# Three-product weight halves for the RWKV columns, branch projections and output projection of a hybrid decoder trunk, with constant matmuls at the norms

## The reference

```python
def swiglu(x, wg, wu, wd):
    return (jax.nn.silu(x @ wg) * (x @ wu)) @ wd
...
    for l in range(DEPTH):
        h = swiglu(rmsnorm(x, P['ffn1_pre_g'][l]), P['ffn1_wg'][l], P['ffn1_wu'][l], P['ffn1_wd'][l])
        x = x + 0.5 * rmsnorm(h, P['ffn1_post_g'][l])
        m, new = token_mix(rmsnorm(x, P['mix_pre_g'][l]), l, P, lb[l], s_rwkv[l], s_shift[l], s_lru[l], s_conv[l], s_hgrn[l])
        x = x + rmsnorm(m, P['mix_post_g'][l])
        h = swiglu(rmsnorm(x, P['ffn2_pre_g'][l]), P['ffn2_wg'][l], P['ffn2_wu'][l], P['ffn2_wd'][l])
        x = x + 0.5 * rmsnorm(h, P['ffn2_post_g'][l])
...
# token_mix
    proj = u @ P['w_in'][l]
    pa, pb, pc, pg = jnp.split(proj, [A_PROJ, A_PROJ + 2 * B_WIDTH, A_PROJ + 2 * B_WIDTH + 2 * C_KWIDTH + 2 * C_WIDTH], axis=-1)
...
    ga, gb, gc = jnp.split(jax.nn.sigmoid(pg), 3, axis=-1)
    merged = ga * (oa @ P['proj_a'][l]) + gb * (ob @ P['proj_b'][l]) + gc * (oc @ P['proj_c'][l])
    return merged @ P['w_out'][l], (n_rwkv, n_shift, n_lru, n_conv, n_hgrn)
```

## Time and profile before

| | |
|---|---|
| median of 3 runs | 2296.34 us (2294.59 to 2296.5) |
| the profiled execution | 2293.74 us, its span 2291.8 us |
| PE busy | 2158.2 us (94%) |
| DVE busy | 1142.8 us (50%) |
| ACT busy | 662.9 us (29%) |
| mean DMA rate | 110 GB/s |
| granted TensorE clock, mean | 0.976 of 2.4 GHz |

### The profile page before, as it was taken

One profiled execution on the slowest core, in us unless ns is written; L12 is line 12 of the kernel. 1 busy time (PEld: TensorE's weight loads), 2 busy tenths in 40 slices (PEclk: granted clock), 3 DMA queues, 4 the chain that ended last, 5 costly groups with the idle time before them and its releaser, 6 DMA issues.

```text
span 2291.8 us, 29515 instructions
## 1 busy us (share of the span) xinstructions
PE 2158.2 (94%) x11960; PEld 1812.0 (79%) x11960; DVE 1142.8 (50%) x1787; ACT 662.9 (29%) x751; POOL 35.9 (2%) x72
## 2 busy tenths in 40 slices
PE   7999899999999997999889997999999999979997
PEld 6999667777766766999889996677776666669996
DVE  5443435776557424444354534366754664254533
ACT  4443231211141203443334333212211321034332
POOL 0000000000000000000000000000000000000000
PEclk9999999999999998999999998999999999989998
DMA  5444231111222332444334442311112323324342
GB/s 196 146 150 162 78 125 59 49 65 47 79 95 95 111 110 94 158 151 150 126 140 155 146 162 78 112 42 66 47 65 79 104 85 112 111 100 157 146 158 85
DMA packets 37624, 251.98 MB, mean 110 GB/s; under 512 B 4672, under 2 KB 4864, under 8 KB 8864
## 3 DMA queue, kind: packets, MB, share of 16 engines
q1 hardware_dynamic: 32688, 234.60, 28.5%
q0 software_dynamic: 4848, 16.13, 1.9%
HBM read 242.05 MB, written 8.67 MB: 109 GB/s over the span
## 4 chain that ended last, share of the span: by engine, by line
PE 84%; DVE 9%; ACT 3%; DVEq 3%; issue 1%; DMA 1%; ACTq 0%; SPq 0%
PE dps L471 41%; PE dps L408 15%; PE dps L425 12%; DVE tmp L997 2%; PE mx L562 2%; PE mx L556 2%; PE mx L564 2%; PE mx L438 1%; ACT tmp L761 1%; DVE x L1000 1%; ACT L761 1%; DVE wlo L994 1%; PE mx L670 1%; PE mx L680 1%; DVEq L1397 1%
## 5 line engine op out<-in xcount | busy, mean ns | idle before, releaser
L994 DVE TENSOR_TENSOR wlo<-raw,whi 128x2048 fp32r<-128x2048 f32 x136 | 311.5, 2292 | 398.6 <-ACT whi L761 391.2
L471 PE MATMUL dps<-uh,whi 128*128 128x320 f32 x1408 | 430.5, 306 | 30.6 <-DVE ul L994 30.6
L471 PE MATMUL dps<-uh,wlo 128*128 128x320 f32 x1408 | 436.9, 310 | 0.0
L471 PE MATMUL dps<-ul,whi 128*128 128x320 f32 x1408 | 435.7, 309 | 0.0
L425 PE MATMUL dps<-u,raw 128*128 128x320 f32 x1280 | 407.7, 445 | 0.0
L761 ACT ACTIVATE whi<-raw 128x2048 fp32r<-128x2048 f32 x136 | 259.8, 1912 | 325.0 <-PE dps L471 325.0
L471 PEld LDWEIGHTS dps<-uh,whi 128*128 128x128 f32 x1408 | 267.1, 190 | 33.1 <-issue 32.6
L425 PEld LDWEIGHTS dps<-u,raw 128*128 128x128 f32 x1280 | 226.8, 193 | 70.0 <-issue 11.9
L471 PEld LDWEIGHTS dps<-uh,wlo 128*128 128x128 f32 x1408 | 267.4, 190 | 0.0
L471 PEld LDWEIGHTS dps<-ul,whi 128*128 128x128 f32 x1408 | 266.6, 189 | 0.0
L471 PE MATMUL dps<-hfh,whi 128*128 128x320 f32 x704 | 221.1, 314 | 0.0
(11 more groups left out here) (249 smaller groups left out, 2229.0 us busy)
## 6 DMA issues: line engine op xcount, KB each, us to landing
raw<-in_wstream SPq DMA_DIRECT2D x220, 1024.0 KB, 4.8
hs<-in_st_hgrn POOLq DMA_DIRECT2D x8, 512.0 KB, 3.6
out_o_hgrn<-hsn POOLq DMA_DIRECT2D x8, 512.0 KB, 2.9
sw<-in_smallw POOLq DMA_DIRECT2D x2, 1024.0 KB, 7.1
ss<-in_st_rwkv POOLq DMA_DIRECT2D x8, 256.0 KB, 4.0
out_o_rwkv<-ssn POOLq DMA_DIRECT2D x8, 256.0 KB, 2.3
x<-in_xT SPq DMA_DIRECT2D x4, 320.0 KB, 4.2
out_yT<-x SPq DMA_DIRECT2D x1, 1280.0 KB, 4.5
```

The source lines that it names most:

```text
L471: m = pe.matmul(dps[:, 2 * half + c, 0:T], w[:, k, c * P:(c + 1) * P], v[:, k0 + k, :], start=first and k == 0 and i == 0, stop=last and k ...
L994: return nc.vector.tensor_tensor(out, a, b, op)
```

## The change

1. The A columns, the branch projections and the output projection go from the full to the split form. The unit of splitting is a **half**: half a block, 8 products, 1024 numbers per partition. There are 34 halves in a layer (0 and 1 the low-rank inputs, 2 to 13 r, k and v, 14 to 25 the branch projections, 26 to 33 the output). `high` copies a half on ACT, `low_half` subtracts on DVE, `half_tiles` and `product` multiply. Rounded and low parts go to rooms in tensors that are idle then, four halves deep: `high` of half h waits until half h-4 has been multiplied. A raw buffer is now free for the next block when its second half has been subtracted. `merged`, `oa`, `ob` and `oc` are split as well; `oa` and `ob` inside the HGRN2 heads, `oc` behind the last head, where also the first four halves of the projections are split. The mixer's `norm_in` now makes `uh` and `ul` too.
2. `keep_busy(n)` puts n matmuls of constants (128 by 256 columns, float32, into a bank that nobody reads then) on PE before and after the norm sums in front of the FFNs and of the mixer.
3. In the first FFN, the first block is rounded before the root instead of after it.

The work of the B, C and gate columns is unchanged. The diff, cut to these parts:

```diff
+            def product(out, h, k, n0, src, first, last):
+                wh, wl = split_half(h)
+                hi, lo_ = src
+                for i, (w, v) in enumerate(((wh, hi), (wh, lo_), (wl, hi))):
+                    m = pe.matmul(out, w[:, k, n0:n0 + P], v[:, k, :], start=first and i == 0,
+                                  stop=last and i == 2, skip_group_check=True)
                 return m
+            def half_tiles(l, h, fresh=False):
+                j, c = half_block(h)
+                pe.wait_ge(S["half_lo"], l * NHALF + (h + 1))
+                if c == 0:
+                    pair_wait(l, (Q_A + j - B_A) // 2, j % 2)
+                for k in range(KD):
+                    if fresh and k % 2 == 0:
+                        u_wait(l, 1, k)
+                    m = product(dps[:, 2 * (j % 2) + c, 0:T], h, k, 0, (uh, ul), k == 0, k == KD - 1)
+                m.then_inc(S["half_done"], 1)
+            def keep_busy(n):
+                for _ in range(n):
+                    pe.matmul(mx[:, 0, 0:2 * P], ident, cst[:, 0:2 * P], start=True, stop=True)
...
+                start = l == f == 0
+                keep_busy(0 if start else 12)
                 norm_sum(l, 4 * f)
+                keep_busy(14 if start else 8)
...
+                keep_busy(12)
                 norm_sum(l, 2)
+                keep_busy(11)
+                for h in range(H_A):
+                    half_tiles(l, h, fresh=h == 0)
...
+            def high(l, h):
+                j, c = half_block(h)
+                if c == 0:
+                    act.wait_ge(w_loaded[j % 2], (l * (NBLK // 2) + j // 2) * 16 + 16)
...
+                if 4 <= h < H_PROJ or h >= H_PROJ + 4:
+                    wait_half(act, l, h - 4)
+                fn(split_half(h)[0], full_half(h), ACT.Copy).then_inc(S["half_hi"], 1)
...
+            def low_half(l, h):
+                hi, lo_ = split_half(h)
+                dve.wait_ge(S["half_hi"], l * NHALF + (h + 1))
+                if h == H_PROJ + 1:
+                    dve.wait_ge(S["ss_free"], (l + 1) * HP + 1)
+                elif h == H_PROJ + 2:
+                    wait_full(dve, l, B_PROJ - 1)
+                tt(lo_, full_half(h), hi.bitcast(F32), ALU.subtract).then_inc(S["half_lo"], 1)
...
+                for h in range(H_PROJ, H_PROJ + 4):
+                    low_half(l, h)
+                low_branch(l, 2)
+                for h in range(H_PROJ, H_OUT):
+                    br, i, part = (h - H_PROJ) // 4, (h - H_PROJ) % 4, h % 2
+                    k = slice(2 * i, 2 * i + 2)
+                    wait_half(dve, l, h)
+                    dst = merged[:, k, :] if br == 0 else xs[:, 0:2, :]
+                    mul(dst, dps[:, 2 * part:2 * part + 2, 0:T], gate[:, 8 * br + 2 * i:8 * br + 2 * i + 2, :])\
+                        .then_inc(pair_free[part], 1)
...
+                    if br == 2 and i > 1:
+                        low_merged(i - 2)
+                    if br < 2 or i < 3:
+                        low_half(l, h + 4)
+                low_merged(2)
+                low_merged(3)
...
+                if start:
+                    squares(l, 0)
...
+                    split_hi(l, 0, 0, 0, f)
+                    root(l, 0)
+                    split_hi(l, 0, 1, 1, f)
```

335 lines of the change are left out of this document (217 added, 118 removed).

## The result

The changed kernel takes **2255.95 us** (median of 4 runs, 2255.02 to 2257.43) against 2296.22 of the kernel before on the same chip: ratio 0.983, 95% interval 0.9817 to 0.9844. The profiled executions have spans of 2253.2 and 2291.8 us. So 40.3 us are gained by the medians and 38.6 by the spans, where 46.9 were forecast; the time lies in the forecast range, 7 us above the predicted 2249.

A forecast was written before the change was run, and what follows sets the result against it. PE was taken as the bound, with 84% of the chain. Terms 18.7 + 22.4 + 3.5 + 2.3 = 46.9 us off 2293.74 gave 2246.8; with 2.6 for the median, 2249 us, range 2238 to 2264.

The forecast's parts named there:

- The pace of the products: In the changed stages: split products take 0.440 us instead of 0.538, at most 53 us over 544 products.
- A columns: Mixer's stretch from first u to first attention product: gains of 8.9 and 9.8 us in the two layers, together 18.7.
- The one stall that the walk through the queues had found: A columns: PE waits 1.3 us before half 2, whose slot's copy stands behind `high` of half 4 and table loads.
- Projections and output: Branch and output projections after the last head: gain of 11.2 us a layer, 22.4 in all.
- the other ten halves end at 833.2: Projections, after the 3.5 us stall behind half 15: remaining projection halves finish at 833.2, at 3.52 us of PE each.
- First block ahead of the root: Start of the first FFN: reciprocal comes earlier than 18.24 when the first block is copied before the root; 3.5 us.
- Constant matmuls: Around norm sums: gain of 2.3 us, 1.1 at layer 0's FFN2, 0.2 at two other starts, 1.0 at the first FFN.
- The rule of the Trainium skill: Low-clock penalty at three later FFN starts: would give back 6.3 us instead of 1.3; the prediction set it aside.
- The constant matmuls did not lose the clock or run late: Rival, 4%: at half clock, constant matmuls push norm sums and first products by up to 5 us at five places: 2274.
- The queues do not couple further: Rival, 15%: late low-rank reads in A and the projections lose 4 to 9 us a layer: 2257 to 2267.
- DVE the pace of the projections: Rival "Slower", 2%: DVE's work per half becomes the pace in projections and output, 40 us lost there: 2312.
- More comes back: Rival, 12%: low clock counts by its full share, or the loop's pace holds and stalls fill: 2236 to 2243.

The follow-up runs named there:

- the fifth run: Changed kernel with ScalarE's three decay-constant functions and their table loads moved between the mixer norm's root and the copies of u: 2254.54 us, ratio 0.9823.
- The sixth run: Changed kernel with 8 constant matmuls on PE ahead of half 16, order on DVE and ACT unchanged: 2254.43 us, ratio 0.9823.
- The third run: Changed kernel with DVE's gate multiplications of halves 14 and 15 ahead of later weight subtractions and the low part of `oc`: 2247.15 us, ratio 0.9793.
- The seventh run: Changed kernel with the first FFN's first block copied behind the root again, as in the kernel before: 2260.84 us, ratio 0.9852.
- The ninth run: 15 constant matmuls instead of 8 at three later FFN starts, against a kernel combining gates first, early table loads and earlier low parts of `merged`: 2238.67 us.
- the eleventh: Six constant matmuls in each layer's first HGRN2-head pause, on a kernel with gates first, early tables, earlier `merged`, second-block subtraction behind the norm: 2230.47 us, ratio 0.9723.
- the fourth run: Changed kernel without the third matmul (low weights by high activations) of each product in the new stages: 2212.43 us, one run.

## Why the prediction was nearly right, and which term was too large

**The pace of the products.** 0.1467 us a record was measured, as forecast, and the full form costs 0.542 a product. Right.

**A columns: forecast 8.9 and 9.8 us, measured 8.5 and 8.85.** The one stall that the walk through the queues had found is there, with its size (1.30 us) and its cause, which the fifth run shows: with the table loads ahead of `u` it closes and A is 1.54 and 1.59 us shorter. Over both layers 1.35 us are missing. Half 0 ends 8.1 us after the first u in layer 0 and not 7.8; the rest is not assigned.

**Projections and output: forecast 11.2 us a layer, measured 9.0 and 8.6.** This is the mis-sized term, 4.8 of the 8.3 us between the forecast and the spans. The wait behind half 15 was forecast at 3.5 and is 3.8 and 3.6. The tail, from the last projection to the first output half's end, was forecast at 5.8 and is 5.7 in layer 0 (825.5 to 831.24). What failed is the step "the other ten halves end at 833.2", which prices half 16 at 3.52 us as if PE came to it at the full clock. PE had paused for 3.8 us, the clock had fallen, and half 16 took 6.3. In layer 1 a shorter low stretch fell on half 16 and a second one behind the tail's pause; they cost 1.8 and 1.6. With the waits that is 3.0 us in layer 0 and 3.5 in layer 1, where 2.2 and 2.6 are missing, so some 0.8 us a layer came out better than forecast elsewhere in the stage; where is not known. The prediction had used this very link (a pause, then a low clock) for the FFN starts, and did not apply it to the new pause that it had itself found. The sixth run separates the two: with the pause filled and the order unchanged, half 16 is done 2.5 us earlier. The third run takes away both wait and low clock and gains 3.8 and 6.0.

**First block ahead of the root: forecast 3.5.** The reciprocal and the first product come 3.8 us earlier than before. The seventh run gives 2.8 of it back, and would give some 3.7 had its norm sum taken the 7.0 us of the changed kernel. The term is right.

**Constant matmuls: forecast 2.3, measured 1.7 by the spans and 4.4 by the medians.** The forecast is near, and its places are wrong, so this is in part luck. At the FFN starts they bring nothing, since 8 of them end 3.7 us before the first product; the step "8 take 3.4 of the 6.47 us idle" counted a cover of half the pause as a cover of it. The ninth run, with the pause filled, gets what had been forecast for layer 0 (0.97 for 1.1). What there is comes at the mixer's norms (1.2 in the two layers), which the prediction had at nothing. At the first FFN the low clock of the kernel before cost 1.0, as forecast, and it is gone. But without constant matmuls it costs only 0.1 there, as the first product comes earlier (PE is busy for 3.5 us at the low clock and not for 5.4); the gain is not theirs alone.

**The rule of the Trainium skill** (TensorE: Matmul & The Clock Gate, Terms: throttled time times the share withheld). At the FFN starts PE is paced by `ul`. The ninth run removed three low stretches of 6.8, 3.4 and 3.4 us and measured 1.3 us for them, where the rule gives 6.8, or 6 if only the time counts in which PE was busy. Behind half 15 nothing paces PE. The clock was low for 6.8 us there and PE busy for 5.7 of them: the rule gives 3.4, half of the busy time 2.8, and 2.5 came back. So the rule is near at that place. The prediction was right to set it aside at the FFN starts and missed this one.

**What nobody forecast: the heads.** They moved by -2.4 and +1.3 us, and by up to 3.5 among the experiments, where their code was the same in all but the eleventh, by the number of low stretches that fall in them. Against the kernel before at an equal count they are longer by 0.7 us in layer 0 (two stretches, 431.7 against 431.0) and by 0.2 to 0.9 in layer 1 (four); the work on `oa` and `ob` and whatever else changed in them costs no more than that. The rest of the -2.4 and the +1.3 is one stretch more and one less. In this kernel a shift of 1 us ahead of them can cost or give 1.5. FFN2 of layer 1 lost 1.1 us; PE was busy for 5.3 us at the low clock at its start, and for 3.7 in the kernel before, whose clock was already 0.86 at 2042 to 2044. Of it 0.35 lies ahead of FFN2's reciprocal, in each changed kernel up to the ninth run. The rest fits the clock: in the ninth run, with no low stretch there, the stage takes 257.6 us, against 257.4 before. That run differs in the stages ahead too, so the clock is the likely cause and not a shown one.

**The rivals.** The constant matmuls did not lose the clock or run late. The queues do not couple further than the named stall in A and the named wait in the projections. Nor is DVE the pace of the projections in the changed kernel: PE is in the chain for 216 records on end. But the fourth run shows how near it is: with a product of two thirds the length, half of the gain goes into that loop. "More comes back" was excluded by the low clock behind half 15.

## What to carry to other kernels

When a change opens a new pause on PE, price the work behind it at the low clock, and not only the pause. Filling a pause with constant matmuls helps only if they reach to its end; half a cover was worth nothing at three places here, a full one was worth what the pace of the supplying engine leaves. A PE row that is busy to 100% does not mean that the clock is up: read the granted clock beside it. And when a gain of 1 or 2 us has vanished from the span, compare stage by stage with the granted clock beside each stage before calling the edit worthless: two of these edits did what they should, and the heads took much of it back. Such a comparison of single executions needs the other executions' times beside it.

## What the runs showed of the hardware that was not expected

The same code took PE 415.1 to 417.5 us in the heads of layer 0, by the number of stretches at 1.2 GHz (the run with constant matmuls in the heads apart). Most of these stretches, 53 of 78, began with PE busy and no pause ahead of them, at or behind a run of matmuls with 8 columns. The clock fell behind some pauses and not behind others of the same length: the tail's pause in the projections (2.07 us of PE idle in each layer) was followed by 1.00 in layer 0 of the changed kernel and by 0.50 in layer 1, and in layer 0 by 0.57 when it came 2.5 us earlier. What decides between them these runs do not settle.
